# A two-block transformer kernel: qkv split without its norm, two norms as one factor, FFNs opened with two panels side by side

## The reference

```
# first block, layer 0: gated mixers, x += ..., then conv_ffn
# first block, layer 1:
h = rms_norm(x, odd_norm_g)
q, k, v = split(h @ w_qkv)            # 1024 -> 3 x 1024
q, k = rotary(q), rotary(k)           # x*cos + swap_halves(x)*sin
x = x + attention(q, k, v) @ w_o
x = conv_ffn(x)                       # rms_norm, @ w_up (1024 -> 2 x 2816), 3-tap conv,
                                      # silu(gate)*val, @ w_down, added to x
x = rms_norm(x, final_norm_g)
# second block: shift, scale, gate = chunks of (silu(c) @ w_ada + b_ada)
h = rms_norm(x, norm_mix) * (1 + scale) + shift
... three mixers from h @ w_in, a gated sum, then 32 experts ...

rms_norm(x, g) = x * rsqrt(mean(x*x) + 1e-6) * g
```

## Time and profile before

| | us |
|---|---|
| median of three runs | 1676.9 (1675.8 to 1677.26) |
| the profiled execution | 1676.46 |
| its span, first to last instruction | 1674.7 |
| PE busy | 1555.6 (93%) |
| DVE busy | 691.7 (41%) |
| ACT busy | 511.4 (31%) |
| POOL busy | 117.7 (7%) |
| mean granted TensorE clock | 0.968 of full speed |

### The profile page before, as it was taken

The page is one execution under the profiler, slowest core; times in us unless marked ns, Lnnn a source line. Parts: engine busy times, 40 slices in busy tenths (PEclk is TensorE's granted clock), DMA queues, the critical chain, the costliest instruction groups (busy, mean ns, idle before and its releaser), DMA issues.

```text
span 1674.7 us, 26947 instructions
## 1 busy us (share of the span) xinstructions
PE 1555.6 (93%) x10672; PEld 1269.1 (76%) x10672; DVE 691.7 (41%) x1296; ACT 511.4 (31%) x831; POOL 117.7 (7%) x50
## 2 busy tenths in 40 slices
PE   7988999989998999989998887998899999999997
PEld 5767999989678999978887876887666655555554
DVE  5945888357566886232414421412311111111111
ACT  2355554354446564352223104202111101111100
POOL 0111122212001122100000000000000000000000
PEclk9989999999999999989999987999799999999999
DMA  7664555745434656514442211354799999999994
GB/s 298 235 261 164 168 168 165 254 137 166 146 115 125 188 182 184 161 50 146 131 126 76 64 38 50 105 155 139 298 428 426 427 428 426 428 425 428 427 427 208
DMA packets 57977, 375.72 MB, mean 224 GB/s; under 512 B 6560, under 2 KB 6816, under 8 KB 42272
## 3 DMA queue, kind: packets, MB, share of 16 engines
q1 hardware_dynamic: 57888, 374.43, 60.6%
HBM read 373.35 MB, written 1.05 MB: 224 GB/s over the span
## 4 chain that ended last, share of the span: by engine, by line
PE 62%; DMA 15%; issue 12%; DVE 6%; ACT 3%; POOL 0%; SPq 0%; POOLq 0%; DVEq 0%; ACTq 0%
PE lin L617 15%; DMA moe_arena<-in_experts 14%; PE lin L598 5%; PE mixp L1145 4%; PE lin L599 4%; PE lin L600 4%; PE mixp L1149 4%; DVE mixers L1700 3%; PE lin L901 2%; PE stat L1169 2%; PE lin L1124 1%; PE stat L598 1%; PE mixp L600 1%; PE mixp L598 1%; PE stat L600 1%
## 5 line engine op out<-in xcount | busy, mean ns | idle before, releaser
L598 PE MATMUL lin<-r_hi,w_hi 128*128 128x256 f32 x1024 | 301.4, 294 | 16.8 <-DVE r_lo L1571 8.9
L599 PE MATMUL lin<-r_lo,w_hi 128*128 128x256 f32 x1024 | 293.7, 287 | 0.0
L600 PE MATMUL lin<-r_hi,w_lo 128*128 128x256 f32 x1024 | 293.6, 287 | 0.0
L617 PE MATMUL lin<-h,ring 128*128 128x256 f32 x1280 | 288.0, 385 | 3.0 <-DVE h L1583 3.0
L617 PEld LDWEIGHTS lin<-h,ring 128*128 128x128 f32 x1280 | 245.8, 193 | 40.7 <-issue 6.9
L598 PEld LDWEIGHTS lin<-r_hi,w_hi 128*128 128x128 f32 x1024 | 200.3, 196 | 22.9 <-issue 9.6
L599 PEld LDWEIGHTS lin<-r_lo,w_hi 128*128 128x128 f32 x1024 | 200.9, 196 | 0.7
L600 PEld LDWEIGHTS lin<-r_hi,w_lo 128*128 128x128 f32 x1024 | 200.5, 196 | 0.0
L1559 DVE TENSOR_TENSOR w_lo<-ring,w_hi 128x1024 fp32r<-128x1024 f32 x126 | 156.0, 1242 | 93.6 <-ACT w_hi L1216 70.1
L2175 DVE TENSOR_TENSOR moe_arena<-moe_arena,mixp 128x256 f32<-128x256 f32 x32 | 13.5, 421 | 353.3 <-ACT moe_arena L1505 353.3
L1216 ACT ACTIVATE w_hi<-ring 128x1024 fp32r<-128x1024 f32 x124 | 130.0, 1050 | 59.8 <-PE mixp L600 54.5
(11 more groups left out here) (378 smaller groups left out, 2332.3 us busy)
## 6 DMA issues: line engine op xcount, KB each, us to landing
moe_arena<-in_experts SPq DMA_DIRECT2D x96, 2048.0 KB, 18.5
ring<-in_panels SPq DMA_DIRECT2D x272, 512.0 KB, 3.6
aring<-in_ada SPq DMA_DIRECT2D x24, 1024.0 KB, 6.3
cst<-in_consts SPq DMA_DIRECT2D x1, 1696.0 KB, 11.7
x<-in_x SPq DMA_DIRECT2D x1, 1024.0 KB, 4.7
out_x<-x SPq DMA_DIRECT2D x2, 512.0 KB, 2.6
mixers<-in_even_w_s SPq DMA_DIRECT2D x1, 512.0 KB, 13.4
colp<-in_cols SPq DMA_DIRECT2D x1, 361.5 KB, 5.1
```

What stands on the lines that cost most here:

```text
L598: pe.matmul(o, w_hi[:, slot, c], r[0], start=start, stop=False, skip_group_check=True)
L599: pe.matmul(o, w_hi[:, slot, c], r[1], start=False, stop=False, skip_group_check=True)
L600: return pe.matmul(o, w_lo[:, slot, c], r[0], start=False, stop=stop, skip_group_check=True)
L617: mm = pe.matmul(lin[b][:, 0:T], w[:, i, :], rhs[:, i, :], start=i == 0, stop=i == k - 1)
```

## The change

Three parts, with what they take along.

1. **qkv rows split without their norm.** `r_hi` and `r_lo` are made of x times the gain, pair by pair behind the residual adds of FFN 0 (`deferred_rows` on ACT, `lower_rows` on DVE), with no norm factor. The factor goes into cos and sin (`cos1`, `sin1`), and into v, whose eight tiles DVE now multiplies out of PSUM in place of ACT's copies. PE does the first qkv panel with the last two pairs' sums between its tiles (`opening_panel`). An FFN does these last sums itself only if it is the second one.
2. **Final and next norm as one factor.** With s the mean of x*x and g the final gain, the mean of the squares of the normed x is (mean of g*g*x*x)/(s + eps), so the two norms in a row need two sums over the same squares: one with ones, one with g*g + eps as weights (`weighted_sum`). Ln of both, one Exp over both. h is x times a gain (norm_mix gain times final gain) times the joint factor; x itself is normed behind it.
3. **Both FFNs begin with two panels side by side**: per channel tile the three products of panel 0, then those of panel 1. Panels 2 and 3 follow as before.

Beside these: the third chunk's columns and gains move from ahead of the second output projection into FFN 1's down stage; and `keep_warm` adds products whose result is not used, 512 columns wide: four ahead of FFN 1, three ahead of the second block's small product.

```diff
+            def weighted_sum(tiles):
+                for m in tiles:
+                    mm = pe.matmul(stat[:, 2, :], gains[:, 2 * KD + m:2 * KD + m + 1].to_broadcast([P, P]), sq[:, m, :],
+                                   start=m == 0, stop=m == KD - 1, skip_group_check=True)
+                if m == KD - 1:
+                    mm.then_inc(sums_ready, 1)
+            def keep_warm(b, count):
+                pe.wait_ge(bank_free[b], panels.free[b])
+                for _ in range(count):
+                    pe.matmul(lin[b][:, :], K["ident"], cst[:, 0:512], start=True, stop=True, skip_group_check=True)
+            def opening_panel():
+                b = split_panel()
+                bank(b)
+                for i in range(KD):
+                    if i == KD - 2:
+                        stream_sum([4, 5])
+                        stream_sum([6, 7])
+                    pe.wait_ge(h_ready, seen(h_ready))
+                    mm = split_matmul(lin[b][:, 0:T], (b, slice(i * P, (i + 1) * P)), (r_hi[:, i, :], r_lo[:, i, :]),
+                                      i == 0, i == KD - 1)
...
-            def ffn(modulated=False):
-                for j in range(4):
+            def ffn(chunks, last):
+                opening = [split_panel(j) for j in (0, 1)]
+                for b in opening:
+                    bank(b)
+                for i in range(KD):
+                    pe.wait_ge(h_ready, seen(h_ready))
+                    for b in opening:
+                        mm = split_matmul(lin[b][:, 0:T], (b, slice(i * P, (i + 1) * P)), (r_hi[:, i, :], r_lo[:, i, :]),
+                                          i == 0, i == KD - 1)
+                        if i == KD - 1:
+                            mm.then_inc(panel_done, 1)
+                for j in (2, 3):
                     b = split_panel(j)
                     bank(b)
-                    split_linear(b, first=j == 0)
+                    split_linear(b)
...
                     if pair >= 2:
                         stream_sum([2 * pair - 4, 2 * pair - 3])
+                        if last and pair == 3:
+                            weighted_sum(range(4))
                 panels.advance_down()
-                for b in (2, 3):
-                    stream_sum([2 * b, 2 * b + 1])
+                if last:
+                    for b in (2, 3):
+                        stream_sum([2 * b, 2 * b + 1])
+                        weighted_sum([2 * b, 2 * b + 1])
...
-            modulation_columns(lin[2], 2)
-            pe.wait_ge(mod_read, 3)
+            pe.wait_ge(modrow_ready, 3)
             project(None)
-            ffn()
-            for m in range(KD):
-                stream_sum([m])
+            keep_warm(panels.n % 4, 4)
+            ffn((2,), True)
+            keep_warm(2, 3)
...
+            def deferred_rows(gain):                    # ACT
+                for b in range(4):
+                    act.wait_ge(bank_free[b], panels.free[b] + 1)
+                    act.activation(sq[:, 2 * b:2 * b + 2, :], x[:, 2 * b:2 * b + 2, :], ACT.Square).then_inc(sq_ready, 1)
+                    for k in (2 * b, 2 * b + 1):
+                        act.activation(r_hi[:, k, :], x[:, k, :], ACT.Copy, scale=gain(k)).then_inc(r_hi_ready, 1)
+                panels.advance_down()
+                split_hi(panels.n + 4)
+                norm_rest(1, D)
...
+            def lower_rows(gain, tiles):                # DVE
+                for k in tiles:
+                    dve.wait_ge(r_hi_ready, seen(r_hi_ready))
+                    dve.scalar_tensor_tensor(r_lo[:, k, :], x[:, k, :], gain(k), r_hi[:, k, :].bitcast(F32), ALU.mult,
+                                             ALU.subtract).then_inc(h_ready, 1)
...
+            link(dve.tensor_tensor(cos1, K["cos"], rs[:, 0, :], ALU.mult))
+            link(dve.tensor_tensor(sin1, K["sin"], rs[:, 0, :], ALU.mult))
...
+            for n in range(8):
+                b = panels.done()
+                dve.tensor_tensor(v1[:, n, :], lin[b][:, 0:T], rs[:, 0, :], ALU.mult).then_inc(bank_free[b], 1)
```

More of the change, by code:

```diff
@@ L701, in ffn @@
                         down(split_panel(j + 2, it), ds(it * 4 + (j + 2), 1), False, False)
-                if modulated:
-                    for chunk in range(2):
-                        pe.wait_ge(bank_free[chunk], panels.free[chunk])
-                        modulation_columns(lin[chunk], chunk)
+                for chunk in chunks:
+                    pe.wait_ge(bank_free[chunk], panels.free[chunk])
+                    modulation_columns(lin[chunk], chunk)
                 for k in range(18, KF - 2):
@@ L802, in _ @@
             qk_first = panels.n
-            for n in range(16):
-                linear(None, 1, first=n == 0)
-                if n:
-                    swap_halves(n - 1)
+            opening_panel()
+            for n in range(1, 16):
+                linear(None, 1)
+                swap_halves(n - 1)
             linear(None, 1)
@@ L1222, in round_rows, with stream_norm @@
                     act.activation(r_hi[:, k, :], h[:, k, :], ACT.Copy).then_inc(r_hi_ready, 1)
-            def stream_norm(first=False, down=False, rows=True):
-                for m in range(0, KD, 2 if down else 1):
-                    if down:
-                        act.wait_ge(bank_free[m // 2], panels.free[m // 2] + 1)
-                    elif not first:
+            def stream_norm(first=False, rows=True):
+                for m in range(KD):
+                    if not first:
                         panels.taken(m)
-                    n = 2 if down else 1
-                    act.activation(sq[:, m:m + n, :], x[:, m:m + n, :], ACT.Square).then_inc(sq_ready, 1)
-                    if not (first or down):
+                    act.activation(sq[:, m, :], x[:, m, :], ACT.Square).then_inc(sq_ready, 1)
+                    if not first:
                         split_hi(min(panels.n + m + 5, panels.n + KD + 2))
-                if down:
-                    panels.advance_down()
-                elif not first:
+                if not first:
                     panels.advance(KD)
@@ L1243, in stream_norm, with final_norms @@
                     split_hi(panels.n + 4)
+            def deferred_rows(gain):
[7 more added lines that the diff above has]
+                norm_rest(1, D)
+            def final_norms():
+                for b in range(4):
+                    act.wait_ge(bank_free[b], panels.free[b] + 1)
+                    act.activation(sq[:, 2 * b:2 * b + 2, :], x[:, 2 * b:2 * b + 2, :], ACT.Square).then_inc(sq_ready, 1)
+                panels.advance_down()
+                act.wait_ge(sums_ready, seen(sums_ready))
+                act.activation(rs[:, 1, :], stat[:, 0, :], ACT.Ln, bias=K["eps"], scale=1.0 / D)
+                act.wait_ge(sums_ready, seen(sums_ready))
+                act.activation(rs[:, 0, :], stat[:, 2, :], ACT.Ln, bias=K["eps_sq"], scale=1.0 / D).then_inc(ln_done, 1)
+                act.wait_ge(ln_done, seen(ln_done))
+                act.activation(rs[:, 0:2, :], rs[:, 0:2, :], ACT.Exp, scale=-0.5).then_inc(rs_ready, 1)
             def norm_rest(groups, width, at=0):
@@ L1344, in _ @@
             for n in range(8):
-                take(v1[:, n, :])
+                panels.done()
+                panels.advance(1)
+                split_hi(panels.n + RING)
             for i in range(HEADS + 2):
@@ L1382, in conv_tiles @@
                 panels.advance(count)
-            stream_norm(down=True, rows=False)
-            for m in range(KD):
-                act.wait_ge(ev("x_final"), m + 1)
-                act.activation(sq[:, m, :], x[:, m, :], ACT.Square).then_inc(sq_ready, 1)
-            norm_rest(1, D)
+            final_norms()
             def shifted(half):
@@ L1831, in conv_tiles @@
                 panels.advance(count)
-            modulated(0)
+            modulated(3 * KD)
+            for k in range(KD):
+                dve.scalar_tensor_tensor(x[:, k, :], x[:, k, :], col("final_norm", k), rs[:, 1, :], ALU.mult, ALU.mult)\
+                    .then_inc(ev("x_final"), 1)
+            dve.wait_ge(ev("x_final"), KD)
             dve.wait_ge(ev("small_ready"), 1)
```

60 lines of the change are left out of this document (34 added, 26 removed).

## The result

Four runs of the changed kernel took 1657.5, 1650.2, 1657.0 and 1658.3 us against 1676.9, 1677.3, 1675.8 and 1679.3 of the kernel before: medians 1657.3 and 1677.1, ratio 0.9871, 95% interval 0.9847 to 0.9895 (the ratio is that of the means, into which the one run of 1650.2 goes in full; the medians alone give 0.9882). The forecast was 1661, with 15.8 us won. Of the executions profiled, 18.9 us were won (1657.52 against 1676.46). One execution of the last experiment's kernel ran at a granted clock of 0.74 and took 1992.7 us; it is left out of that kernel's median.

What follows compares the result with a forecast made beforehand. TensorE was taken as the bound (62% of the span), with gains where it stands still or runs at the lower clock. Terms 7.0 + 2.36 - 0.9 + 1.4 + 2.7 - 2.0 + 5.2 = 15.8 gave 1661 us, range 1655.5 to 1667.

Steps and rivals of the forecast that it cites:

- the deferred norm: Between first FFN's down stage and qkv: first qkv panel done at 352.5 instead of 359.54, 7.0 us won.
- both of its covers: At qkv's start: last r_lo ready with 1.8 us of slack; ACT's panel copy at 355.2, wanted at 355.4.
- the columns: Modulation columns moved from ahead of second projection into down stage: 2.36 us won, 0.9 paid, 1.4 for the clock.
- the second FFN's opening: Two panels side by side, four wide products ahead: both panels end at 523.4 instead of 526.1, 2.7 us won.
- the loss in the first FFN: Opening with two panels delays ACT's first tap; the loop hangs on DVE, so 2.0 us lost.
- the merged norm: Final and next norm as one factor: modulated scaling at 720.2 instead of 725.39, 5.2 us won.
- (a): Rival, chance 0.14: filler does not hold the clock and the dip at 486 stays; less 1.4 and 2.4, 1664.9 us.
- (c): Rival, chance 0.10: the first FFN's loop swallows the late tap; 2.0 us more won, 1659 us.
- (d): Rival, chance 0.07: second FFN's loop falls into the first's slow turn, margin 0.5 us; 11.4 lost, 1672.5 us.
- (e): Rival, chance 0.03: DVE, held by GpSimd, bounds second FFN and qkv; 24.6 lost against 15.8 won, 1685.8 us.
- (b): Rival, chance 0.14: the clock stays up through the final norm; 4.3 us more won, 1656.8 us.
- a microsecond won before 728 us arrives at the end whole: Next block waits for the same products and expert loads start once its panels are used, so earlier gains carry through.

Runs made afterwards that it cites:

- the last experiment's kernel: Changed kernel with GpSimd's panels moved by two places up to qkv, plus all large DMA targets at multiples of 512 bytes: 1649.5 us, ratio 0.9836.
- the repeat of before: The kernel before run once more, nothing edited: 1676.5 us.
- The second series: The changed kernel and the kernel before run again, nothing edited: 1657.8 against 1675.4 us, ratio 0.9897, interval 0.9882 to 0.9912.

## Why the prediction was right, and where it was wrong

Right, each by its own stretch in the first table: the deferred norm (7.19 for 7.0), with both of its covers; the columns (2.36, 0.87 paid, 1.49 for the clock, returned exactly when undone); the second FFN's opening (2.65 for 2.7); the loss in the first FFN (2.13 for 2.0) and its cause, VectorE held by GpSimd; the merged norm (8.81 us from first sum to scaling, 8.8 forecast). GpSimd's margin in the second FFN held. Of the rivals, (a), (c), (d) and (e) are refuted by these stretches. Of (b), the clock did stay up through the norm, but it fell in the small product in every trace with the filler, and of its 4.3 us 0 to 1.3 came, by the run. The clock's term for the columns is part luck: the repeat of before would have given 2.7 instead of 1.5, and by its own row (0.58 of full speed over 4 us) it was 1.7 rather than 1.4.

Wrong: the step "the block behind these waits for the same products ... so a microsecond won before 728 us arrives at the end whole", and with it the sum. The microseconds won before 728 us did arrive; what failed is that everything behind 728 us was priced at nothing, as if the change touched nothing there. 3.5 us stood there in the experts' loads, which the diff's line `gains = sb("gains", [P, 4 * KD])` brought: it moved the arena that they write to a multiple of 256 bytes. I had read that line as storage for two more rows of factors and not asked what lies behind it, although the chain gave DMA 15%. With this term the forecast is 1661 - 3.5 = 1657.5, where the medians are (1657.3, 1657.8).

The rest is the clock: the changed kernel has either length of each stretch in one run or another. Several stretches behind 728 us have two or three lengths, by the run. Since two traces were compared, 3.0 us won and 3.5 lost there look like effects and are not; together they lost 0.5. The range's lower end, 1655.5, is 0.9872 of before. The first series' ratio lies just under it at 0.9871, and takes both to get there: the 3.5 us of the loads, and the one run of 1650.2, without which it would be 0.988. Why that run was so fast stays open. The second series' ratio, 0.9897, lies in the range.

A smaller error inside a term that came out right: "the full clock alone would not help" in the second FFN. It gives 1.0 us (129.59 to 128.57). And one reading was wrong where the term came out right, "it did not rise during the small product": in the trace of before the clock was full when the small product began at 726.56, and fell in it. It reads 1.00 from 726 to 728 us and 0.50 from 730 to 735; over both:

```profile
726.00:733.00 7.00, 6.42 (x32) 6.07 (x32) 2.65 (x7) 3.21 (x8) 0.00 (x0) 0.66 0.00 0
```

## What to carry to other kernels

A diff that adds or widens a tile moves all tiles behind it: where a stage is bound by DMA, look at where the tiles that it writes begin, and put them at multiples of 256 bytes (0.7% of that stage here). When an engine's part of a shared job is dealt out by slot number, the same slot falls on another place of the turn in each loop; choose the slot for each loop by what the other engine does just then. And compare stretches between landmarks rather than totals: a term of 2 us was read to 0.1 us that way where the totals scattered by 8.

## What the runs showed of the hardware

- Loads of 2 MB into SBUF: 430 GB/s where the destination begins at a multiple of 256 bytes, 427 where it is off by 64, 128 or 192; 3.5 us over 201 MB (the 192 MB of the experts' weights, counted in millions of bytes).
- Four products of 4 columns (eight rows of the profile) with 0.97 us of standstill ahead and 1.3 behind went with half clock in all four traces that had them. 1.23 us of standstill in front of the second FFN, behind wide products, did not: the clock stayed full.
- The fp32 small product (16 columns, 5.2 to 6.8 us) went with half clock in all 18 traces. Behind 0.9 to 1.2 us of standstill with wide products ahead of it, the clock fell 1.2 to 4.2 us after its start; behind 3.5 us (the kernel before) 1.7 us after its start; in the one trace with 3.8 us, 1.6 us ahead of it.
- VectorE's cast of one tile took 0.28 us by itself and up to 2.24 beside a GpSimd subtraction. It cost 1.04 us per turn where it was the last of a turn (12.56 us against 11.52), and nothing in the middle of one (11.45).
- Stretches of one program have two or more lengths from run to run (27.0 or 28.7, 119 or 122.7 us; 142.3 to 150.1 at the start), by where the granted clock rises or falls.
